# Key norms of a recurrent branch: a power on GpSimd in place of a root on ScalarE and a reciprocal on VectorE

## The reference

```
k_k: weights, k: projected and shifted keys, heads of 64
kk = heads(k * k_k)
kk = kk / max(sqrt(sum(kk * kk, axis=-1)), 1e-12)
k_mod = k * (1 + (a - 1) * k_a)
bonus = sum(r * k_mod * r_k, axis=-1) * v
```

## Time and profile before

| what | us |
|---|---|
| median of 3 runs | 1636.12 (1632.76 to 1644.48) |
| the profiled execution | 1635.15 |
| its span | 1633.4 |
| TensorE busy | 1503.9 (92%) |
| VectorE busy | 711.0 (44%) |
| GpSimd busy | 405.3 (25%) |
| ScalarE busy | 351.5 (22%) |
| the front, from TensorE's first product to its last | about 412 to 679 |

### The profile page before, as it was taken

The page is one execution under the profiler, slowest core; times in us unless marked ns, Lnnn a source line. Parts: engine busy times, 40 slices in busy tenths (PEclk is TensorE's granted clock), DMA queues, the critical chain, the costliest instruction groups (busy, mean ns, idle before and its releaser), DMA issues. The chain is left out here.

```text
span 1633.4 us, 30007 instructions
## 1 busy us (share of the span) xinstructions
PE 1503.9 (92%) x12303; PEld 920.1 (56%) x12303; DVE 711.0 (44%) x1433; ACT 351.5 (22%) x687; POOL 405.3 (25%) x480
## 2 busy tenths in 40 slices
PE   7999998989999999899999998999998399999992
PEld 4664455455887888787888885443554133333320
DVE  4203044433255467584756662446565222222225
ACT  3002144454123323000212111121112111111122
POOL 3001056654200000104983320002221321111124
PEclk9999999999999999999999998999999599999996
DMA  6613299999432311546442325444302799999996
GB/s 233 229 38 116 78 311 341 382 352 344 145 131 85 109 53 38 114 120 153 127 100 81 90 68 191 141 170 147 138 29 74 244 313 414 393 396 409 402 318 239
DMA packets 117210, 320.96 MB, mean 196 GB/s; under 512 B 30264, under 2 KB 48120, under 8 KB 106288
## 3 DMA queue, kind: packets, MB, share of 16 engines
q1 hardware_dynamic: 89696, 244.47, 41.6%
q0 software_dynamic: 26080, 70.26, 13.6%
q10 hardware_dynamic: 1296, 4.29, 0.7%
HBM read 268.52 MB, written 58.30 MB: 200 GB/s over the span
## 5 line engine op out<-in xcount | busy, mean ns | idle before, releaser
L1213 PE MATMUL rw_pp<-rows,rw_w 128*128 128x264 f32 x960 | 217.7, 387 | 0.0
L1213 PEld LDWEIGHTS rw_pp<-rows,rw_w 128*128 128x128 f32 x960 | 181.6, 190 | 33.4 <-issue 2.8
L1617 PE MATMUL gate_p<-rows,gate_w 128*128 128x264 f32 x520 | 124.7, 394 | 6.3 <-DVE u_rw L1946 5.0
L2533 PE MATMUL x_p<-wgu,rows 128*32 128x512 f32 (+1 forms) x640 | 124.0, 610 | 2.3 <-ACT rows L2551 1.3
L2533 PE MATMUL x_p<-late,rows 128*32 128x512 f32 (+1 forms) x640 | 122.6, 599 | 0.0
L1617 PEld LDWEIGHTS gate_p<-rows,gate_w 128*128 128x128 f32 x520 | 98.9, 193 | 25.7 <-DVE u_rw L1946 6.2
L1572 POOL DMA_DIRECT2D t_ring<-t_blocks x128 | 69.4, 550 | 81.6 <-DVE tt L1833 73.9
L490 POOL DMA_INDIRECT rows<-in_cache_kT,page_index x41 | 42.2, 1029 | 187.2 <-PE fox_b L546 100.1
L2560 DVE SCALAR_TENSOR_TENSOR obT<-x_p,moe_ent,late 128x1024 f32<-128x1024 f32 x24 | 30.8, 1284 | 116.7 <-PE x_p L2545 116.7
L2510 POOL DMA_INDIRECT y<-obT,moe_ent x24 | 24.4, 1017 | 228.8 <-DVE obT L2560 215.5
L2551 ACT ACTIVATE rows<-h_p,vec 128x128 f32<-128x128 f32 x96 | 27.5, 369 | 247.9 <-PE h_p L2528 247.9
(11 more groups left out here) (507 smaller groups left out, 2660.7 us busy)
## 6 DMA issues: line engine op xcount, KB each, us to landing
wgu<-in_we_gu SPq DMA_DIRECT2D x16, 2048.0 KB, 17.4
late<-in_we_gu SPq DMA_DIRECT2D x16, 2048.0 KB
wd<-in_we_down SPq DMA_DIRECT2D x16, 1024.0 KB, 7.6
late<-in_we_down SPq DMA_DIRECT2D x16, 1024.0 KB
rows<-in_cache_kT SPq DMA_DIRECT2D x41, 256.0 KB, 5.3
gate_w<-in_w_in SPq DMA_DIRECT2D x38, 256.0 KB, 3.0
gate_rows<-u_rw SPq DMA_DIRECT2D x72, 132.0 KB, 2.8
y<-const SPq DMA_DIRECT2D x9, 1024.0 KB, 6.3
```

Source lines behind the costliest of these rows:

```text
L1213: mm = pe.matmul(pp[u % 2][:, c, 0:QN], w[:, n % 2, k, :] if n else e.w_first[:, k, :], e.xnT[:, k, at:at + QN], start=(i == 0), stop=(i = ...
L1617: mm = pe.matmul(bank, weights_at(pair, name)[:, k], moving[g][:, k], start=(k == 0), stop=(k == half_k - 1))
L2533: mm = pe.matmul(gu[d][at:at + n, :], hT[:, d, k, at:at + n], wgu[u][:, k, :], start=(k == 0), stop=(k == KD - 1))
```

## The change

The root on ScalarE and the reciprocal on VectorE go. GpSimd gets a column of the constant -0.5 and raises `t2` to that power in place, once per pair, behind its four multiplications. VectorE waits for the power (`inverted`) where it took the reciprocal. The semaphore `rt` gives way to `inverted`, which the memset raises too, so pair `p` waits for `p + 2`.

```diff
+            pool.memset(power[:], -0.5).then_inc(inverted, 1)
+            for p in range(HP):
+                pool.wait_ge(ss_max, p + 1)
+                pool.wait_ge(inverted, p + 1)
+                pool.tensor_tensor(t2[:], t2[:], power[:].to_broadcast([P, NT]), ALU.pow).then_inc(inverted, 1)
...
-                if u in at_s:
-                    p = at_s[u]
-                    act.wait_ge(ss_max, p + 1)
-                    act.activation(t2[:], t2[:], ACT.Sqrt).then_inc(rt, 1)
...
                 dve.tensor_scalar(quarters(t2[:]), banks, 1e-24, None, ALU.max).then_inc(ss_max, 1)
                 shift(3 + 2 * p, spare[1])
-                dve.wait_ge(rt, p + 1)
-                st.then(dve, dve.reciprocal(t2[:], t2[:]))
+                dve.wait_ge(inverted, p + 2)
                 dve.wait_ge(shifted, 4 + 2 * p)
```

More of the change, by code:

```diff
@@ L1077, in stage_rwkv_front @@
     made_z, made_a, sq_done, made_s = sem("rw_made_z"), sem("rw_made_a"), sem("rw_sq"), sem("rw_made_s")
-    ss_max, rt, exps, rk_ready, made_b, sum_kept = (sem("rw_ss_max"), sem("rw_root"), sem("rw_exps"),
+    ss_max, inverted, exps, rk_ready, made_b, sum_kept = (sem("rw_ss_max"), sem("rw_inverted"), sem("rw_exps"),
                                                     sem("rw_rk"), sem("rw_made_b"), sem("rw_sum_kept"))
@@ L1098, in stage_rwkv_front @@
         keep = sb("keep", [P, NT], BF16)
-        over_sums = sb("over_sums", [H * TT, P])
+        over_sums, power = sb("over_sums", [H * TT, P]), sb("minus_half", [P, 1])
         pp = [ps(f"rw_pp{b}", [P, 2, 512]) for b in range(2)]
```

## The result

The changed kernel takes 2263.97 us (median of 4 runs, 2260.38 to 2266.84) against 1637.28 us of the kernel before in the same measurement: a ratio of 1.383 (95% interval 1.379 to 1.387), 627 us more. The forecast was slower, 1717 us, in a range from 1632 to 1830 us. The direction held, and so did the way in which a power makes TensorE wait; the length of the power did not, and with it the size.

The account below looks back on a forecast made before the run. TensorE was taken to bound the front, with one 2.3 us wait. The profiled 1635.15 us plus 69.7 of waiting and 11.2 of lower clock gave 1716.1, about 1717 us by the median; range 1632 to 1830 us.

Parts of the forecast that it names:

- What bounds the kernel: In the front (400 to 720 us) TensorE is the bound, waiting once, 2.3 us, for VectorE's line 1348 in pair 0.
- The chain and its sum: Each pair's late power delays TensorE's head sums by 18.0 us; four add up, less 2.29 us: 69.7 us.
- D: Duration of one GpSimd power of 128x1056, one per pair; forecast 28.5 us.
- the formula as I wrote it: Added time: four times D less 10.5 us, less the 2.3 us wait already there, plus 11.2 us for the clock.
- The limit: Longest power that leaves TensorE unwaiting: 10.5 us taken, 13.4 us if the shift lies beside the power.
- the shift: VectorE's 2.86 us shift of the next column block, between maximum and reciprocal; forecast ahead of or behind the power.
- The collision that I read from the earlier trace: GpSimd and VectorE wait for each other's whole instruction; a 0.17 us cast took 1.22 us beside a GpSimd multiplication.
- The clock: After each 18 us TensorE stop, 5.6 us of work at half speed, 2.8 us lost; four pairs 11.2 us.
- The length of the power: GpSimd power priced as two curves of 13.05 us, each like a reciprocal, plus a 2.42 us multiplication: 28.5 us.
- the upper bound of 56 us: For one power: GpSimd's page-index row scaled to 1056 columns, 10.4 us, times VectorE's reciprocal ratio of 5.4.
- beyond 56 us: Case of a still longer power, such as one worked out one partition at a time; unbounded by rows, chance 0.17.
- the forecast's own lower end: Bottom of the forecast case's range, about 1646 to 1771 us, for a power of 13 to 42 us; chance 0.38.

Follow-up runs that it names:

- Two kernels that remove it: Changed kernel with one multiplication by a constant for the power: 1631.87 us; kernel before with pair 0's reciprocal ahead of the shift: 1634.97 us.
- the last run: Kernel before plus an end block of seven GpSimd powers (1056, 600, 528 columns), one VectorE operation started into each: 2664.21 us.
- the third experiment: Changed kernel with eight multiplications in a row in place of each power: 1665.39 us, ratio 1.0159.
- the fourth: Changed kernel with the power on columns 0 to 527 only, the rest multiplied by a constant: 1938.20 us, ratio 1.1822.
- The first experiment: Kernel before plus an end block of GpSimd powers run alone, then six of 264 columns beside VectorE operations: 2330.22 us.

## Why the prediction was wrong

*What bounds the kernel* was right: TensorE, with the one wait of 2.3 us. Two kernels that remove it win 2.5 us in the stretch.

*The chain and its sum* were right: four waits of D less a limit, which add up; nothing else late; a lower clock after each stop. With the measured D the formula as I wrote it gives 4 x (169.2 - 10.5) - 2.3 + 11.2 = 643.7 us against the 629.6 of the spans, 2% off.

*The limit* was mis-taken: 10.5 us where the runs show 13.3 to 13.7, since the shift lies beside GpSimd's work where that is long enough or comes in several instructions. That is 11 us of the sum. The collision that I read from the earlier trace rows is real, but in pairs 1 to 3 it held one instruction for 82 us, and the shift then ended long before the power. Only in pair 0 of the changed kernel was an instruction held to the power's end, as I had it; there the limit was 11.8 us. The Trainium skill ("SBUF — State Buffer", on the engine ports) has the lock last for a whole instruction; the copies of the last run agree (167.64 of 168.45 us), and so does pair 0's copy; but the addition with two inputs got through after 82 of 168 us, and beside 528 columns was not held at all, so here the measurement goes before the page.

*The clock* cost 8.0 us where I took 11.2: behind its stops of 156 us 1.7 to 2.2 us each. Behind the stops of 4.4 us of the third experiment and those of 73 us of the fourth the rows take 2.6 to 2.9 us more, near the 2.8 that I had taken from the earlier trace rows. So the length of the stop does not explain the difference, and this stays open.

*The length of the power* is the step that failed: 28.5 us forecast, 169.2 measured, six times as much, and three times the upper bound of 56 us. 4 x (169.2 - 28.5) = 563 us, more than the whole of the 547 us by which the forecast fell short; the limit and the clock pull the other way by 14. The 28.5 us and the bound were both built on the assumption that a curve on GpSimd costs what a reciprocal costs on VectorE in multiples of a plain operation, and the 28.5 us also on a power being two such curves and a multiplication, which no run shows. The first experiment shows no such relation: 87 multiplications, where 28.5 us were 12 of 2.42 us and 56 us were 23. The bound was not one by its own rule either: an addition of 30 columns on GpSimd (line 1536, at 838.25 us) took 0.48 us (0.26 the other time), 0.016 us a column against 0.0098 for the page index, which gives 91 us by the same steps, and that is still too short. The prediction said that D is in no row, and gave "beyond 56 us" a chance of 0.17; the range should have been left open at the top, for no row bounded it. (A small slip beside it: 1646 us as the forecast's own lower end leaves out the 2.3 us; D of 13 us gives 1644 us, or 1655 with the clock. Nothing hangs on it.) The Trainium skill's factor of about two for elementwise work on GpSimd ("GPSIMD Engine Reference", on its performance against VectorE) agrees with a multiplication of two full tiles (2.35 us for 1024 columns against 1.25 for 1056 on VectorE); the multiplication by one column takes 1.94 us alone. Of this operation it says nothing: the 0.160 us per column have no counterpart there.

## What to carry to other kernels

An operation that no row of a profile shows has no upper price: measure it alone, at two sizes, before anything waits for it. Here one probe would have told that a power on GpSimd costs 0.160 us per column, for 16 partitions as for 128, so a tile of 1056 columns is far too wide for it while 16 columns take 2.9 us. And look first at what there is to win: the wait was 2.3 us, and moving the reciprocal ahead of a shift that waits anyway removes it without a new engine, though 2.5 us are too few to be told from no change in the time of this kernel.

## What the runs showed of the hardware

A GpSimd power takes 0.160 us per column, alike for 16 and 128 partitions, for float32 and bf16, for -0.5 and 2, for a constant and for data. Beside it VectorE is not held by one rule: an addition with two SBUF inputs waits until about 82 us into a power of 600 or 1056 columns, and beside 264 or 528 not at all or little (0.98 us for 0.17 at the start of a power of 528 in the fourth experiment); a copy from SBUF to SBUF, of all columns or of 8, waits to the end beside 1056, and a copy of all columns does not wait beside 264; a copy of one column (line 1313 in pair 0, 0.15 us, 6 us into the power) did not wait; a reciprocal or an operation that reads PSUM went on as if alone. Why is open. And a stop of TensorE of 4.4 us cost 7.2 us, since the eight matmuls and the unit behind it ran at the lower granted clock (0.50) in part.
